# The first x piece issued from ScalarE's queue, its high part made by VectorE, six warm-up products instead of seven

## The reference

```
h = rms_norm(x, attn_norm)            # x * rsqrt(mean(x^2)) * gain
proj = h @ w_in                       # 1024 x 6144, cut into q_r k_r v_r g_r q_m k_m v_m
o_r  = group_norm(retention(rotary(q_r), rotary(k_r), v_r)) * silu(g_r)
o_m  = moba_attention(rms_norm(q_m), rms_norm(k_m), v_m)
x = x + (sigmoid(..) * (o_r @ w_ret_o) + sigmoid(..) * (o_m @ w_moba_o)) @ w_out
u = causal_conv(rms_norm(x, ffn_norm) @ w_up)
x = x + (silu(u_gate) * u_val) @ w_down
```

## Time and profile before

| | us |
|---|---|
| times of 3 runs | 451.52, 453.43, 451.98 |
| median | 451.98 |
| span of the profiled execution, first to last instruction | 450.2 |
| PE busy in the span | 446.6 |

### The profile page before, as it was taken

The page is one execution under the profiler, slowest core; times in us unless marked ns, Lnnn a source line. Parts: engine busy times, 40 slices in busy tenths (PEclk is TensorE's granted clock), DMA queues, the critical chain, the costliest instruction groups (busy, mean ns, idle before and its releaser), DMA issues.

```text
span 450.2 us, 6345 instructions
## 1 busy us (share of the span) xinstructions
PE 446.6 (99%) x2477; PEld 390.5 (87%) x2477; DVE 337.6 (75%) x395; ACT 286.3 (64%) x384; POOL 102.6 (23%) x69
## 2 busy tenths in 40 slices
PE   9999999999999999999999999999999999999997
PEld 6899988888888999999999888888888888888886
DVE  4789994876699839673368578589999999987423
ACT  6885453055996759233425368499999999996300
POOL 0100021499360021210000003333433333300000
PEclk9999999999999999999999999999999999999999
DMA  8997658557999425997555553977787778873102
GB/s 278 422 406 255 251 190 234 141 186 204 258 268 310 177 94 181 278 317 254 188 188 190 184 187 113 318 247 234 233 242 233 239 245 243 252 250 128 58 0 93
DMA packets 61385, 98.70 MB, mean 219 GB/s; under 512 B 48048, under 2 KB 48944, under 8 KB 52016
## 3 DMA queue, kind: packets, MB, share of 16 engines
q1 hardware_dynamic: 60944, 96.79, 67.6%
q0 software_dynamic: 416, 1.57, 1.0%
HBM read 85.77 MB, written 1.05 MB: 193 GB/s over the span
## 4 chain that ended last, share of the span: by engine, by line
PE 99%; DVE 0%; issue 0%; POOL 0%; POOLq 0%
PE bank L558 8%; PE bank L560 8%; PE bank L559 8%; PE bank L751 8%; PE bank L750 8%; PE bank L749 8%; PE bank L511 6%; PE bank L512 6%; PE bank L510 6%; PE bank L796 4%; PE bank L794 4%; PE bank L793 4%; PE bank L697 2%; PE bank L696 2%; PE bank L695 2%; PE bank L524 2%
## 5 line engine op out<-in xcount | busy, mean ns | idle before, releaser
L1079 DVE TENSOR_TENSOR w_pair<-w_raw,w_pair 128x2048 fp32r<-128x2048 f32 x73 | 176.4, 2437 | 47.2 <-ACT w_pair L813 46.9
L813 ACT ACTIVATE w_pair<-w_raw 128x2048 fp32r<-128x2048 f32 x73 | 139.0, 1924 | 30.9 <-PE bank L560 13.3
L749 PE MATMUL bank<-w_pair,h_hi 128*128 128x512 f32 x160 | 62.2, 389 | 0.0
L750 PE MATMUL bank<-w_pair,h_hi 128*128 128x512 f32 x160 | 62.2, 389 | 0.0
L751 PE MATMUL bank<-w_pair,h_lo 128*128 128x512 f32 x160 | 62.2, 389 | 0.0
L558 PE MATMUL bank<-a_hi,w_pair 128*128 128x256 f32 x192 | 53.8, 280 | 0.0
L559 PE MATMUL bank<-a_lo,w_pair 128*128 128x256 f32 x192 | 53.6, 279 | 0.0
L560 PE MATMUL bank<-a_hi,w_pair 128*128 128x256 f32 x192 | 53.6, 279 | 0.0
L510 PE MATMUL bank<-w_pair,h_hi 128*128 128x512 f32 x128 | 49.9, 390 | 0.0
L511 PE MATMUL bank<-w_pair,h_hi 128*128 128x512 f32 x128 | 49.8, 389 | 0.0
L512 PE MATMUL bank<-w_pair,h_lo 128*128 128x512 f32 x128 | 49.8, 389 | 0.0
(11 more groups left out here) (162 smaller groups left out, 853.6 us busy)
## 6 DMA issues: line engine op xcount, KB each, us to landing
w_raw<-weights_dram SPq DMA_DIRECT2D x73, 1024.0 KB, 5.8
w_raw<-weights_dram SPq DMA_DIRECT2D x8, 256.0 KB, 5.2
w_raw<-weights_dram SPq DMA_DIRECT2D x4, 512.0 KB, 8.8
ys<-x_dram SPq DMA_DIRECT2D x2, 512.0 KB, 8.9
xs<-x_dram POOLq DMA_DIRECT2D x1, 1024.0 KB, 5.4
area<-decay_dram SPq DMA_DIRECT2D x1, 768.0 KB, 8.8
out_dram<-ys SPq DMA_DIRECT2D x3, 256.0 KB, 2.0
xs<-x_chan_dram SPq DMA_DIRECT2D x1, 512.0 KB, 6.7
```

Of the source, the lines that this page charges most:

```text
L749: mm(o, s_hi, hi[:, kk, :], start=(k == 0), stop=False)
L750: mm(o, s_hi, lo[:, kk, :], start=False, stop=False)
L813: A(w_parts(n, r)[0], raw[r][:, :], ACT.Copy).then_inc(hi_ready, 1)
L1079: tt(lo, raw[r][:, :], hi.bitcast(f32), ALU.subtract).then_inc(lo_ready, 1)
```

## The change

ScalarE's queue issues x piece 0, ahead of ACT's table load. SP's list then begins with quarter 0 of half 0, and all else in it moves up by one place. The high part of slice 0 is made by DVE (a tensor_scalar multiply) in place of ACT, with a semaphore of its own, for which PE and DVE's own xg_low wait. ACT makes no xg_high for slice 0 and does not wait for x piece 0 until slice 1. Six warm-up products are made in place of seven.

```
-WARM_UP = 7
+WARM_UP = 6
...
+        xg_first_ready = sem("xg_first_ready")
...
+        def wait_xg_hi(eng, k):
+
+            eng.wait_ge(xg_hi_ready if k else xg_first_ready, max(k, 1))
...
             def load_x_chan(c, piece):
                 k0, k1 = X_PIECES[c]
-                a, z = 2 * KT + SEQ * k0 if k0 else 0, 2 * KT + SEQ * k1
-                sp.dma_start(x_head[:, a:z], piece).then_inc(x_chan_loaded[c], 16)
-
-            load_x_chan(0, x_chan0)
+                sp.dma_start(x_head[:, 2 * KT + SEQ * k0:2 * KT + SEQ * k1], piece).then_inc(x_chan_loaded[c], 16)
+
             load_quarters(0, 0)
             load_quarters(1, 0)
...
                     if b == V_R0:
-                        pe.wait_ge(xg_hi_ready, k + 1)
+                        wait_xg_hi(pe, k)
...
+            act.dma_start(x_head[:, 0:2 * KT + SEQ], x_chan0).then_inc(x_chan_loaded[0], 16)
             nc.scalar.preload_act_table(ACT.Square)
...
             for c, (k0, k1) in enumerate(X_PIECES):
-                act.wait_ge(x_chan_loaded[c], 16)
+                if c:
+                    act.wait_ge(x_chan_loaded[0], 16)
+                    act.wait_ge(x_chan_loaded[c], 16)
                 for k in range(k0, k1):
-                    xg_high(k)
+                    if k:
+                        xg_high(k)
...
+            def xg_high_first():
+                ts(xg_hi[:, 0, :], x_t[:, 0, :], gain_col[:, 0:1], None, ALU.mult).then_inc(xg_first_ready, 1)
+
             def xg_low(k):
-                dve.wait_ge(xg_hi_ready, k + 1)
+                wait_xg_hi(dve, k)
...
             for c, (k0, k1) in enumerate(X_PIECES):
                 dve.wait_ge(x_chan_loaded[c], 16)
+                if c == 0:
+                    xg_high_first()
```

## The result

| | median us | lowest to highest | executions |
|---|---|---|---|
| before | 452.25 | 451.50 to 453.71 | 20 |
| changed | 453.70 | 452.07 to 454.58 | 20 |

What follows compares the result with a forecast made beforehand. PE's work was taken to bound the kernel; about 0.2 us gained at the start would be lost waiting at half 5, except 0.1 us from half 4 landing earlier: 451.98 - 0.1 = 451.9 us, range 451.1 to 453.2.

Steps and rivals of the forecast that it cites:

- What bounds the kernel: Whole span: PE is busy 99%, without a gap from 34 us to 400, so only its earlier shift counts.
- The wait at half 5: Near 33 us PE waits 0.12 us for DVE's low part; this would grow to 0.32 and take the gain.
- When the first quarter lands: Start: the first weight quarter lands at 3.2 us in place of 3.58, near the lower bound of 3.11.
- The sum at the start: First product at 3.95 in place of 4.35 us; PE about 0.2 us earlier everywhere behind 6.4 us.
- Rival D: Start: a pause after warm-up puts off the clock's rise, each us costing 0.5 us; up to 454.6; chance 0.05.
- the missing product: Warm-up: one product less frees PE 0.43 us earlier, at 3.71; dropping a product of zeros costs nothing.
- Half 4 landing earlier: Weight stream: half 4 stands behind the same bytes and lands 0.1 us earlier, ends 0 and 0.33.
- the forecast's own sign of being wrong: In the profile after: the prediction is wrong if half 4 lands as much earlier as the issues do.
- The high part on VectorE: Slice 0 at the start: takes 0.35 us on DVE, 0.65 at the other end; saves ACT 0.51 us.
- B: PE's gain at the start is carried to the end, 0.2 to 0.43 us won, 451.55 to 451.8; chance 0.17.
- C: Start: the two transfers share the engines, both land near 3.5, PE begins at 4.3; 452.0 us; chance 0.09.
- E: Outside the span: using ACT's queue costs 0 to 1.5 us at launch or end, up to 453.4; chance 0.07.

Runs made afterwards that it cites:

- six_only: Kernel before with six warm-up products in place of seven; 453.67 us against 452.53, ratio 1.0018.
- sp_swapped: Changed kernel with seven warm-up products and SP issuing the first quarter, then x piece 0, on one queue; 452.40 us against 452.35, ratio 1.0001.
- before_warm9: Kernel before with nine warm-up products; 452.36 us against 452.35, ratio 0.9998.
- high_only: Changed kernel with SP issuing x piece 0 first again and seven warm-up products; 452.64 us against 452.53, ratio 1.0002.
- low_first: Kernel before with nine warm-up products, VectorE making half 5's low part ahead of the normalised x; 452.77 us against 452.30, ratio 1.0010.
- queue_only: Kernel before with only the issue of x piece 0 moved to ScalarE's queue, seven warm-up products; 454.17 us against 452.53, ratio 1.0027.
- after_warm8: Changed kernel with eight warm-up products; 452.25 us against 452.30, ratio 1.0002.
- after_warm10: Changed kernel with ten warm-up products; 452.47 us against 452.35, ratio 1.0002.
- after_warm11: Changed kernel with eleven warm-up products; 452.38 us against 452.53, ratio 0.9994.
- quarter_on_act: Changed kernel with ten warm-up products, SP issuing x piece 0 and ScalarE's queue the first quarter; 452.62 us against 452.30, ratio 1.0009.
- act_alone: Changed kernel with seven warm-up products, SP issuing nothing until x piece 0 has landed; 454.70 us against 452.35, ratio 1.0053.
- piece1_late: Kernel before with nine warm-up products, ScalarE's queue issuing x piece 1 only after x piece 0 has landed; 453.01 us against 452.25, ratio 1.0015.
- piece1_on_act: Kernel before with x piece 1 issued from ScalarE's queue, seven warm-up products; 453.73 us against 452.30, ratio 1.0027.

## Why the prediction was wrong

**What bounds the kernel.** Right as far as it went: nothing behind 34 us moved (PE is busy for 364.00 of the 364.00 us from 36 to 400), and the whole difference lies in the first 10 us. The wait at half 5 is real and varies: it is there in the traces of before, six_only, sp_swapped and before_warm9 (up to 0.4 us), and not in those of high_only and low_first. That it is what swallows an arrival some tenths earlier fits, and no run shows it.

**The step that failed: "When the first quarter lands".** The forecast took 3.2 us, between bounds of 3.11 and 3.58, on the reasoning that the quarter "no longer stands behind the other piece on its queue but shares with it". Its first reader began at 4.69, and at 4.28 to 4.74 in the traces of queue_only, after_warm8, after_warm10, after_warm11 and quarter_on_act. The bounds counted latency and bytes, each from one trace. With one queue the same transfers come at 3.50 and 3.85 in sp_swapped, and the quarter at 3.58 to 3.96 in the order of before, so the upper bound was some tenths low there already; the rest, up to 0.8 us, needs the second queue. The bounds did not allow that two queues starting together slow the first packets of both: 19 to 114 GB/s from 1.75 to 2.5 us, against 150 to 262. The Trainium skill's section "Issuing engines are not separate DMA queues" ("DMA: Bandwidth & Descriptors"), quoted in the forecast, speaks only of shared engines and saved issue time; it promised little gain, and the runs show a loss.

**The sum at the start** hence had the wrong sign: first product 1.1 us later, not 0.4 earlier.

**Rival D was the mechanism, with 0.05.** Its form was right (a pause puts off the clock's rise, each microsecond costs half), and its pause wrong: 0.25 to 0.5 us forecast, 1.75 measured. The rise came 3.7 us later in the profiled execution, and together with the late start that is 2.3 us. The mistake behind the chance was to read the pause of before, 0.2 us in one trace, as harmless distance. six_only shows how near the edge it was: one product less, with landings on time and a pause of 1.0 us in the trace, puts 8 of 11 executions over 453.2. So two parts of the change, each alone, cost most of what the whole costs: the queue (ratio 1.0027) and the missing product (1.0018). They do not add up (1.0029), as one would expect if both act through the same late rise. The forecast's second failed term is therefore the missing product, put at nothing: it said that dropping a product of zeros costs nothing, by the Trainium skill's budget of time ("TensorE: Matmul & The Clock Gate", Part 1). six_only measured 0.18%. The rule says that the rise is not bound to a number of products, and the runs agree: with no pause it came between 4.9 and 7.1 us. It does not say that a gap in PE's work is free.

**Half 4 landing earlier.** Forecast 0.1 us, measured 0.88: a term mis-sized. It is more than the scatter. ScalarE's first read of half 4 lies at 22.60 to 23.59 us in the six traces in which SP alone issues these transfers. It lies at 21.74 to 22.29 in eight of the nine with one of them on ScalarE's queue, act_alone left out, and at 23.46 in the ninth. The forecast had half 4 held by the bytes queued ahead of it, and sized the gain by the loose stretch at the start. What moved was its issue, 0.95 us earlier: SP waits there for VectorE's low part of the last quarter of half 0, which was done that much sooner. From the issue to ScalarE's read it is 10.3 to 10.5 us in all these traces but piece1_late (9.2). So the forecast's own sign of being wrong came, half 4 landing as much earlier as its issue. It gave nothing in the changed kernel, because PE was last.

**The high part on VectorE:** 0.35 us as taken, no cost, no gain (high_only 1.0002).

**Rivals B, C, E.** B needed an earlier start, which never came. C had the two transfers landing near 3.5; they came a microsecond later. E, a cost outside the span, is out for these executions: time less span is 454.52 - 452.5 = 2.0 us for the profiled execution; an execution of before timed beside the experiments has 452.58 - 450.7 = 1.9.

**Left open.** Why packets of two queues that start at the same moment are slow for half a microsecond. The runs show only that it needs both, and that it is mild when the second queue carries x piece 1 (161 and 172 GB/s). And what share of executions a given pause lengthens: it may depend on the work before the pause as well, and no rule is drawn from these few.

No version here is faster than the kernel before. Nine warm-up products in it leave the median where it was (0.9998) and had none over 453.2 in 12, where the kernel before had 2 in 30 beside them; that is too few to call a gain.

## What to carry to other kernels

A warm-up should reach past the latest moment at which the first real work can begin, not the median one: spare products of zeros cost nothing that was measurable here (two more in the kernel before, ratio 0.9998), and one too few cost 1.1 us in the median. Before the first transfers are spread over two queues, look at when both start moving; on one queue, back to back, both of the same two pieces were there 0.8 us sooner (3.85 against 4.69). And when a forecast rests on one trace, ask which of its pauses varies from execution to execution and what lies one step beyond it.

## What the hardware did that was not expected

Two queues issuing at 0.73 us together, one with x piece 0 and one with the first quarter, moved 19 to 114 GB/s between 1.75 and 2.5 us in six traces; one queue alone moved 150 to 262 in eight. A transfer that ScalarE's program issues behind its table load went out at 0.76, while the 1.28 us load was running (piece1_on_act). And PE's clock, up at 6.31 us behind a pause of 2.2, fell again at about 7.5 for some three microseconds although PE was at work (act_alone: 0.54 of full speed granted from 7.9 to 11). With a pause of 0.75 us at 8.9, when the clock had long been up, the products behind it still ran at 0.23 us each (piece1_late).
